# A fused encoder block on one core: each expert block's rows gathered and turned one block ahead, and one modulation sum moved behind a projection

## The reference

```python
mod = silu(c) @ w_ada + b_ada                 # sh1, sc1, gt1, sh2, sc2, gt2
h = rmsnorm(x) * (1 + sc1) + sh1
q, k, v, u, vv = split(h @ w_in)              # u, vv through gelu, vv through a layer norm
y = sig(g_a) * (attention(q,k,v) @ w_branch_a) + sig(g_b) * (gating(u,vv) @ w_branch_b)
x = x + gt1 * rmsnorm(y @ w_out)
h = rmsnorm(x) * (1 + sc2) + sh2
top_v, top_i = top_k(h @ w_router + b_router, 4)      # 4 of 32 experts for each token
for each expert e and each token it got:
    gu  = h_tok @ w_gate_up[e] + b_gate_up[e]         # 1024 x 2048
    act = min(gu[:1024], 7) * sigmoid(1.702 * ...) * (clip(gu[1024:], -7, 7) + 1)
    out[tok] += gate * (act @ w_down[e] + b_down[e])  # 1024 x 1024
x = x + gt2 * rmsnorm(out)
```

## Time and profile before

| what | us |
|---|---|
| median of 3 runs (1193.82 to 1199.39) | 1195.16 |
| the profiled execution | 1199.1 |
| its span, first to last instruction | 1196.8 |
| PE busy | 1039.2 (87%) |
| DVE busy | 295.1 (25%) |
| ACT busy | 179.7 (15%) |
| HBM, mean over the span | 388 GB/s |

### The profile page before, as it was taken

One profiled execution on the slowest core, in us unless ns is written; L12 is line 12 of the kernel. 1 busy time (PEld: TensorE's weight loads), 2 busy tenths in 40 slices (PEclk: granted clock), 3 DMA queues, 4 the chain that ended last, 5 costly groups with the idle time before them and its releaser, 6 DMA issues.

```text
span 1196.8 us, 21565 instructions
## 1 busy us (share of the span) xinstructions
PE 1039.2 (87%) x8299; PEld 503.4 (42%) x8301; DVE 295.1 (25%) x813; ACT 179.7 (15%) x453; POOL 31.3 (3%) x54
## 2 busy tenths in 40 slices
PE   4979999978786999899989998999899989697966
PEld 3837888533341343334333433343334333233322
DVE  4644655232110112111211121112111211111112
ACT  3212240121110101101110111111111111001102
POOL 1001001210000000000000000000000000000000
PEclk9989999978896999999999999999999999788977
DMA  9897944989999969999999999999999999999995
GB/s 351 320 374 293 350 172 153 422 343 412 423 425 424 390 277 427 423 428 425 425 427 425 424 425 428 424 405 426 425 427 412 428 423 426 427 422 427 425 424 230
DMA packets 61484, 464.91 MB, mean 388 GB/s; under 512 B 5900, under 2 KB 10060, under 8 KB 28568
## 3 DMA queue, kind: packets, MB, share of 16 engines
q1 hardware_dynamic: 60736, 462.47, 93.7%
q0 software_dynamic: 336, 1.07, 0.2%
q10 hardware_dynamic: 392, 1.09, 0.2%
HBM read 462.50 MB, written 2.11 MB: 388 GB/s over the span
## 4 chain that ended last, share of the span: by engine, by line
PE 68%; DMA 20%; DVE 5%; issue 4%; ACT 2%; DVEq 0%; SPq 0%; POOL 0%; ACTq 0%
PE pp L1539 26%; DMA arena<-in_w_down_dram 17%; PE pp L1568 14%; PE pp L1503 5%; PE pp L1325 5%; DMA arena<-in_w_ada_dram 3%; PE pp L1247 3%; PE pp L1338 2%; PE po L1400 2%; PE pp L1512 2%; PE po L1484 2%; PE pp L1518 1%; PE pp L1257 1%; ACT work L720 1%; DVE work L1094 1%
## 5 line engine op out<-in xcount | busy, mean ns | idle before, releaser
L1539 PE MATMUL pp<-arena,work 128*32 128x256 f32 (+1 forms) x3840 | 387.2, 458 | 20.1 <-ACT work L720 20.1
L1539 PEld LDWEIGHTS pp<-arena,work 128*32 128x32 f32 (+1 forms) x3840 | 169.0, 120 | 222.6 <-issue 140.5
L1568 PE MATMUL pp<-arena,work 128*32 128x256 f32 (+1 forms) x1920 | 198.4, 458 | 52.8 <-DMA arena<-in_w_down_dram 52.8
L1568 PEld LDWEIGHTS pp<-arena,work 128*32 128x32 f32 (+1 forms) x1920 | 77.0, 121 | 153.4 <-issue 68.1
L1091 DVE TENSOR_SCALAR work<-pp 128x128 f32<-128x128 f32 (+1 forms) x74 | 25.0, 338 | 418.9 <-PE pp L1539 418.9
L1503 PE MATMUL pp<-h_sb,work 128*32 128x256 f32 (+1 forms) x480 | 72.3, 528 | 39.6 <-issue 35.2
L723 ACT ACTIVATE work<-work 128x128 f32<-128x128 f32 (+1 forms) x74 | 25.9, 350 | 416.2 <-DVE work L1091 416.2
L1085 DVE COPY work<-pp 128x256 f32<-128x256 f32 (+1 forms) x37 | 19.4, 526 | 246.4 <-PE pp L1503 246.4
L1484 PE MATMUL po<-work 64*128 64x512 f32 x304 | 75.5, 615 | 1.2 <-ACT work L739 1.2
L1503 PEld LDWEIGHTS pp<-h_sb,work 128*32 128x32 f32 (+1 forms) x480 | 23.2, 132 | 84.0 <-issue 78.6
L1325 PE MATMUL pp<-arena 128*128 128x256 f32 x256 | 57.1, 382 | 0.0
(11 more groups left out here) (224 smaller groups left out, 627.6 us busy)
## 6 DMA issues: line engine op xcount, KB each, us to landing
arena<-in_w_gate_up_dram SPq DMA_DIRECT2D x128, 2048.0 KB, 27.6
arena<-in_w_down_dram SPq DMA_DIRECT2D x32, 2048.0 KB, 32.3
arena<-in_w_down_dram SPq DMA_DIRECT2D x64, 1024.0 KB, 19.4
arena<-in_w_ada_dram SPq DMA_DIRECT2D x11, 2048.0 KB, 14.2
arena<-in_w_in_dram SPq DMA_DIRECT2D x4, 2048.0 KB, 19.2
arena<-in_w_gate_dram SPq DMA_DIRECT2D x4, 2048.0 KB, 12.6
arena<-in_w_out_dram SPq DMA_DIRECT2D x2, 2048.0 KB, 10.6
arena<-in_w_ada_dram SPq DMA_DIRECT2D x2, 1024.0 KB, 13.4
```

Source lines behind the costliest of these rows:

```text
L1539: mm = t_.matmul(pp[j * m:(j + 1) * m, UP[hh], 0:w].rearrange("p (s f) -> p s f", s=2), hgT[:, at:at + m], gu_w[slot][:, k, :, r * PAIR:(r ...
L1568: mm = t_.matmul(pp[j * m:(j + 1) * m, UP[0], 0:w], actT[:, at:at + m], wd[:, j * w:(j + 1) * w], start=(n == 0), stop=(n == KD - 1))
```

## The change

Four things are done.

1. `page_rows("vv")` comes before `modulation_sum(2)` on PE, and DVE's multiplication of `gain1` comes after the statistics of `vv`.
2. A block's gather and turn are issued in the block before it: `gather(it + 1, TOKS)` ahead of the fifth k step of the down pass, `turn_rows(it + 1)` ahead of the seventh. DVE's tables for the next block and its copy `take_rows`, and ACT's copy of `hgT`, move with them. The last block does this for a block that doesn't exist.
3. The gathered rows always have the 64-row form: four matmuls of 512 columns, four transposes, copies of 512 columns, in narrow blocks too.
4. The first block's gather and turn stand before the expert loop; `rank` is worked out before the block counts for that. A block now opens with one of the four matmuls of `combine`, the other three stay after the gate-up pass. The biases are issued by `hh` first. DVE reads the next expert's number inside each block.

The diff, cut to what the prediction speaks of:

```diff
@@ ACT @@
+            act.wait_ge(s_turn, 1)
+            a.copy(hgT, pp[:, TURN, :]).then_inc(s_turned, 1)
...
                 def block_of(m, it, halves):
-                    act.wait_ge(s_turn, it)
-                    a.copy(hgT[:, 0:w], pp[:, TURN, 0:w]).then_inc(s_turned, 1)
...
                     a.copy(selgT.rearrange("p t n -> p (t n)"), pp[:, TOKS, 0:TT * P]).then_inc(s_selTev, 1)
+                    act.wait_ge(s_turn, it + 1)
+                    a.copy(hgT, pp[:, TURN, :]).then_inc(s_turned, 1)
                     act.wait_ge(s_y, it)
@@ DVE @@
             modulation(2)
-            dve.wait_ge(s_adasum, 3)
-            dve.wait_ge(s_gain[1], 16)
-            v.tensor_tensor(gain1, gain1, flat2(mod_bank(2)), ALU.mult).then_inc(s_mod_v, 1)
             dve.wait_ge(s_projev, 9)
             modulation(3)
...
                 v.bn_aggr(meanvar[:, t, :], stats[:, t, :]).then_inc(s_mv, 1)
+            dve.wait_ge(s_adasum, 3)
+            dve.wait_ge(s_gain[1], 16)
+            v.tensor_tensor(gain1, gain1, flat2(mod_bank(2)), ALU.mult).then_inc(s_mod_v, 1)
             dve.wait_ge(s_lnsq, 1)
...
+            def take_rows(it, bank):
+                dve.wait_ge(s_hg, it)
+                v.tensor_copy(hg, pp[:, bank, :]).then_inc(s_hgs, 1)
+
+            first = slice(0, 1)
+            select_rows(iota[:, 0:TB], first)
             counts = ...
...
+            take_rows(1, UP[1])
+            select_gates(iota[:, 0:TB], first)
...
             def blocks(nb, wide, n):
...
-                    dve.wait_ge(s_selT, it)
-                    select(iota[:, bass.ds(b * TB, TB)], e)
+                    past = dve.snap((b + 1) // nb, min_val=0, max_val=1)
+                    next_b = dve.snap((b + 1) % nb, min_val=0, max_val=NBLK - 1)
+                    next_n = dve.snap((past + n) % NEXP, min_val=0, max_val=NEXP - 1)
+                    next_e = dve.value_load(tabs[0:1, 2, bass.ds(next_n, 1)], min_val=0, max_val=NEXP - 1)
                     with dve.If(b < wide):
                         block_of(TB, it, halves)
                     with dve.Else():
                         block_of(NARROW, it, halves)
+                    dve.wait_ge(s_selT, it + 1)
+                    select_rows(iota[:, bass.ds(next_b * TB, TB)], bass.ds(next_e, 1))
+                    select_gates(iota[:, bass.ds(next_b * TB, TB)], bass.ds(next_e, 1))
+                    take_rows(it + 1, TOKS)
@@ PE @@
+            page_rows("vv")
             modulation_sum(2)
-            page_rows("vv")
             page_T("u")
             modulation_sum(3)
...
+            def gather(it, bank):
+                pe.wait_ge(s_sel, it)
                 for t in range(TT):
                     for j in range(2):
+                        mm = t_.matmul(pp[j * TB:(j + 1) * TB, bank, :], sel[:, t, :], h_sb[:, t, j * 512:(j + 1) * 512],
+                                       start=(t == 0), stop=(t == TT - 1))
+                mm.then_inc(s_hg, 1)
+
+            def turn_rows(it):
+                pe.wait_ge(s_hgs, it)
+                for i in range(4):
+                    mm = t_.transpose(pp[:, TURN, i * P:(i + 1) * P],
+                                      hg[:, i // 2 * PAIR + i % 2:(i // 2 + 1) * PAIR:2], ident[:])
+                mm.then_inc(s_turn, 1)
+
+            gather(1, UP[1])
+            pe.wait_ge(s_ysb, 2)
+            turn_rows(1)
...
                 pe.wait_ge(s_bgu[slot], landed * 2)
-                pe.wait_ge(s_sel, it)
-                for t in range(TT):
...
+                combine(it, ((0, 0),))
...
-                combine(it)
+                combine(it, ((0, 1), (1, 0), (1, 1)))
...
                 for n, k in enumerate(order):
+                    if n == 2:
+                        pe.wait_ge(s_aTev, halves[1])
+                    if n == 4:
+                        pe.wait_ge(s_selTev, it)
+                        gather(it + 1, TOKS)
+                    if n == 6:
+                        turn_rows(it + 1)
                     if k in (4, 6):
                         pe.wait_ge(s_dhi[k // 2 - 2], dhi_landed)
```

More of the change, by code:

```diff
@@ L1057, in _, with select_rows, select_gates @@
             dve.wait_ge(s_const, 7)
+            link(v.scalar_tensor_tensor(out=rank[:], in0=pp[:, 2, RANK:COUNT].rearrange("p (t e) -> p t e", t=TT),
+                                        scalar=1.0, in1=chosen, op0=ALU.add, op1=ALU.mult))
+            link(v.tensor_scalar(rank[:], rank[:], -1.0, None, ALU.add))
+            def select_rows(places, e):
+                for t in range(TT):
+                    ins = v.tensor_scalar(sel[:, t, :], places, rank[:, t, e], None, ALU.is_equal)
+                ins.then_inc(s_sel, 1)
+            def select_gates(places, e):
+                for t in range(TT):
+                    for c in range(2):
+                        ins = v.tensor_scalar(selg[:, t, c, :], places, rank[:, t, e], gate_tab[:, t, e], ALU.is_equal,
+                                              ALU.mult)
+                ins.then_inc(s_selg, 1)
+            def take_rows(it, bank):
[3 more added lines that the diff above has]
+            select_rows(iota[:, 0:TB], first)
             counts = pp[:, 2, COUNT:COUNT + NEXP].rearrange("p (e a) -> p e a", a=1).to_broadcast([P, NEXP, 8])
@@ L1098, in block_of, with blocks @@
                     v.tensor_tensor(x_sig, x_lin, x_sig, ALU.mult).then_inc(s_actv, 1)
-            def select(places, e):
-                dve.wait_ge(s_tabs, 1)
-                for t in range(TT):
-                    ins = v.tensor_scalar(sel[:, t, :], places, rank[:, t, e], None, ALU.is_equal)
-                ins.then_inc(s_sel, 1)
-                for t in range(TT):
-                    for c in range(2):
-                        ins = v.tensor_scalar(selg[:, t, c, :], places, rank[:, t, e], gate_tab[:, t, e], ALU.is_equal,
-                                              ALU.mult)
-                ins.then_inc(s_selg, 1)
-            def blocks(nb, wide, e):
+            def blocks(nb, wide, n):
                 with dve.Fori(0, nb) as b:
@@ L1144, in _ @@
             with dve.Fori(1, NEXP) as n:
-                nb, wide, e = place_of(bass.ds(n, 1))
-                blocks(nb, wide, bass.ds(e, 1))
+                nb, wide = place_of(bass.ds(n, 1))
+                blocks(nb, wide, n)
             dve.wait_ge(s_x1b, 16)
@@ L1474, in _, with combine @@
             mm.then_inc(s_gT, 1)
-            pe.wait_ge(s_bd, 32)
             pe.wait_ge(s_h2, 2 * TT)
-            pe.wait_ge(s_nblk, 1)
-            def combine(it, last=False):
-                pe.wait_ge(s_ysb, it + 1)
+            def gather(it, bank):
+                pe.wait_ge(s_sel, it)
                 for t in range(TT):
                     for j in range(2):
-                        mm = t_.matmul(po[:, 2 * t + j, :], selgT[j * TB:(j + 1) * TB, t, :],
-                                       y_sb[j * TB:(j + 1) * TB, :], start=False, stop=last, skip_group_check=True)
-                    if last:
+                        mm = t_.matmul(pp[j * TB:(j + 1) * TB, bank, :], sel[:, t, :], h_sb[:, t, j * 512:(j + 1) * 512],
[10 more added lines that the diff above has]
+            turn_rows(1)
+            pe.wait_ge(s_bd, 32)
+            pe.wait_ge(s_nblk, 1)
+            pe.wait_ge(s_tabs, 1)
+            def combine(it, parts, last=False):
+                pe.wait_ge(s_ysb, it + 1)
+                for t, j in parts:
+                    mm = t_.matmul(po[:, 2 * t + j, :], selgT[j * TB:(j + 1) * TB, t, :],
+                                   y_sb[j * TB:(j + 1) * TB, :], start=False, stop=last, skip_group_check=True)
+                    if last and j:
                         mm.then_inc(s_fin, 1)
```

34 lines of the change are left out of this document (6 added, 28 removed).

## The result

The changed kernel takes 1216.97 us (median of 4 runs, 1214.11 to 1220.36) against 1196.18 for the kernel before on the same chip: a ratio of 1.0178, 95% interval 1.0144 to 1.0211. It is 21 us slower. The prediction was 1192.3 us with a range from 1186 to 1200; it was wrong, and the rival that came true is C (PE becomes the bound, 1213). The profiled execution took 1214.11 us, of which 1211.8 are its span. It was the fastest of its four runs while the profiled execution of before (1199.1 us) was a slow one of its kernel, so the two traces differ by 15.0 us where the medians differ by 20.8.

A forecast was written before the change was run, and what follows sets the result against it. PE bounds the mixer, then from 196.3 us the stream of expert weights bounds; -8.8 + 2.5 + 0.5 + 1.0 + 1.9 = -2.9 us gives 1196.2 us profiled, 1192.3 us as a median, range 1186 to 1200.

The forecast's parts named there:

- Rival C: Groups of five blocks: PE becomes the bound and the stream gets a 5.5 us hole per group, 1213 us; chance 0.08.
- A block in the stream: Expert loop: heads shorter, down passes longer, +2.0 us net per group against 3.5 of waiting; 0.5 us lost (0 to 4).
- The modulation sum behind vv: Mixer front on PE: issuing `vv` before the third modulation's sum fills a gap, gaining 8.8 us (7.1 to 9.5).
- The opening of the first block: Start of the expert loop: gate-up starts 1.3 to 2.1 us later, a load hole follows; 2.5 us lost (1.4 to 3.5).
- The hole at 417 to 440 us: Load hole at the expert with two wide blocks: grows by 1.0 us (0 to 2).
- The end: Last block: head gains 0.5 us, gather and turn for a nonexistent block cost 2.4; net +1.9 us (1 to 2.5).
- the mode change: Narrow down pass cut by gather and turn: tiling changes cost up to 0.8 us a block, 1.6 us reaching the time.
- signs of error: Wrong if PE gaps at 100 us, stream holes at 440 to 1180 us, or gather and turn over 2.9 us unwaited.

The follow-up runs named there:

- number 5: The changed kernel with the next block's gather right behind the down pass and its turn behind the opening `combine` matmul: 1185.73 us, ratio 0.9922.
- number 4: The changed kernel plus three (wide) or six (narrow) bf16 matmuls with unused results at each block's end: 1194.81 us, ratio 0.9986.

## Why the prediction was wrong

**"A block in the stream" is the step that failed**, in its net of "+2.0 us net, against 3.5 us of waiting that is there". The second number was right (3.8). The first came out as 10.8 (12.3 - 5.0 + 3.5), by these parts:

- The sum itself was 1.2 us short. By the step's own ends four down passes cost 4 x 2.4, two heads behind wide blocks give 2 x 0.6 and three behind narrow ones 3 x 1.75 in the middle: 3.2 and not 2.0.
- "In the down pass 1.85 (gather) and 0.55 (turn) come in": measured 2.8 in a narrow and 2.5 in a wide block, and 1.5 in the fifth block, whose pass had run partly at half speed before; 12.3 us in all, where I had 9.6. I had left out the fifth because it waits for weights. Its wait did go, but a cost that eats a wait is part of the 3.8 us, and counting it as free beside them counted them twice.
- "behind a narrow block [...] 1.0 to 2.5 less": from narrow to narrow the head shrank from 4.18 us (794.02 to 798.20) to 3.64 (803.91 to 807.55). The gather, the turn and its copies took 2.0 us and went, the opening matmul brought 1.05, and the stand grew by 0.4, from 1.59 us with no semaphore late to 1.97 us for ACT's three copies (the rows are below). From narrow to wide the head gave 0.5 us at one boundary, where the low clock reached into the head itself, and 3.0 at the other, where before a cold gather of 3.5 us stood. All five heads of a group gave 5.0 us, where the net of 2.0 had needed 7.6 (4 x 2.4 - 2.0).
- Nothing in this step was set down for the clock. The rows in it were there: before, a gate-up pass behind a narrow block in the same group takes 9.07 us, not 7.5. The two wide passes of the group, at full clock before, cost 3.5 us more.

The heads from narrow to narrow, first of before, then of the changed kernel:

```profile
795.61 1.07 PE L1503 MATMUL pp<-h_sb,work 128*32 128x256 f32 x16 [1.59 <-issue]
...
798.20 9.07 PE L1539 MATMUL pp<-arena,work 128*32 128x256 f32 x128 [0.46 <-ACT work L720]
```
```profile
805.89 1.12 PE L1518 MATMUL po<-work 64*128 64x512 f32 x2 [1.97 <-ACT work L742]
```

Rival C had this chain, threshold included ("it decides from 3.5 us net per group"), and its 1213 us is 4 us under the median. That it came so near is partly luck: C has no term for the clock, without which a group would overrun by 3.5 us and not by its 5.5, and the 5 us that it adds for the places outside the groups are not there (besides the 8.9 us of the front they came to some 2 us less). I gave it 8 in 100, though my own margin was 1.5 us and the heads behind narrow blocks alone had ends 1.5 us apart, three times a group. With their low ends the group would have stood at 4 x 2.4 - 2 x 0.6 - 3 x 1.0 = +5.4, on the other side of the threshold.

**"The modulation sum behind vv"** was right to 0.1 us at its own place (8.9 for 8.8). It brought the time of the whole down by 6 to 8 us.

**"The opening of the first block"** lost 3.0 us where 1.3 to 2.1 were predicted for gate-up's start. The gather began 0.6 us later than worked out (243.83 against 252.1 - 8.9), the loop's opening cost 2.17 us, inside its 1 to 2.6, and the opening matmul took 2.02 us with 1.7 predicted. The clock came back only in gate-up: 3.8 us at 0.50, then 0.98.

```profile
254.20:258.00 3.80, 3.80 (x44) 0.50 0.74 306
258.00:262.00 4.00, 4.00 (x72) 0.98 0.46 117
```

Gate-up became 0.7 us shorter (9.31 for 10.04 us). That is the direction of the Trainium skill's rule that activity releases the throttle (TensorE: Matmul & The Clock Gate, "What's actually happening"), and no more: counted from the gather on, the clock came back after some 14 us (243.83 to 258), where it had taken 9 in the kernel before, and now there is a stand of 2.17 us in between. No run here separates what the stand did. The term didn't fall to 0.

**"The hole at 417 to 440 us"** was to grow by 1.0 and shrank by 2.6 us. SP's two marks around it did move apart, by 1.7 us (409.78 to 429.67, and 419.38 to 437.57 before), as the gather ahead of the second mark lets expect. But at the first mark the DMA engines still had loads, at 434 GB/s from 409 to 411 us, where before they had run dry (37 GB/s from 417 to 419 us).

**"The end"** came as predicted, +2.2 us for +1.9. From the end of the last but one down pass (1177.35, before 1164.52) to the end of the span it is 34.5 us instead of 32.3: the head is 1.1 shorter (3.73 for 4.85), gate-up 0.5 longer, and the last down pass, which waits for no weights, has the useless gather and turn in it:

```profile
1195.87 1.94 PE L1496 MATMUL pp<-h_sb,work 128*64 128x512 f32 x8
```

On the mode change: the Trainium skill (TensorEngine Tiling (Array Packing), "Key Properties") says that changing the tiling mode drains the engine, and I had worked out up to 0.8 us a block by it. The narrow down pass has four such changes now: 6.47 - 3.66 = 2.81 us, of which the starts at 747.84, 749.71, 750.71 and 751.38 give 1.87 to the gather and 0.67 to the turn. 0.27 us is left for all four, so the trace has a small price here and no more.

Of what I had named as signs of error, one showed: holes in the stream between 440 and 1180 us. Gather and turn stayed just under their sign, with 2.8 us in a narrow block against 2.9, and PE had no gap at 100 us.

## What to carry to other kernels

When a stream and an engine run within a few per cent of each other, the change per period has to be compared with the slack per period, and the range has to be made of both sides of that threshold: under it an edit costs nothing, over it each microsecond comes back once a period. Work that needs nothing is worth more at the place where the engine would wait than in a place where it is busy: moving the gather and the turn from the down pass to the boundary took 31 us off the time without removing an instruction. Ask of each instruction put at the head of a list what it waits for, and what used to run during that wait.

## What the runs showed of the hardware

- One 64-row matmul of 512 columns alone takes as long as two side by side: 1.12 and 1.13 us. So a pair that is split costs a step more.
- The granted clock fell to near 0.5 behind a stand of 1.7 us and a few thin matmuls, too (one `combine` matmul, biases with a 4-row contraction), but not each time. Wide gate-up passes of 15.4 us or more (13.95 is full clock), of 14: the change 12; with a pair in place of the one matmul, and the same stand, 6; with the stand filled by bf16 matmuls, and the one matmul, 5; with both, 0; with the gather in the stand (number 5), 0. What decides in a single block wasn't separated: at 455.01 us of the changed kernel a pass ran at full clock behind the same stand and matmuls.
- Added work can make a kernel faster: the bf16 matmuls of number 4 took 22 us off, with gate-up passes of 379.5 us in all instead of 406.4.
